# Weight slots as separate buffers at four different places within 512 bytes, in a hybrid mLSTM, retention and FFN layer on one core

## The reference, cut to what matters

```
h    = rmsnorm(x, g_mix_pre)
proj = h @ w_in                       # 2048 x 8208: q, k, v, gates of 8 mLSTM and 8 retention heads
mix  = concat(mlstm heads, retention heads) @ w_out            # 2048 x 2048
x    = x + rmsnorm(mix, g_mix_post)
h    = rmsnorm(x, g_ffn_pre)
ff   = (silu(h @ w_gate) * (h @ w_up)) @ w_down                # 2048 x 5632 twice, 5632 x 2048
x    = x + rmsnorm(ff, g_ffn_post)
```

## The kernel before, in words

| buffer | before | after |
|---|---|---|
| raw | 128 | 128 |
| w_hi, slots 0, 1, 2, 3 | 128, 128, 128, 128 | 128, 256, 384, 0 |
| w_lo, all slots | 128 | 0 |
| resid, columns, right, stat | 128 | 0 |
| hT, mixT, wg_both, qT, kT, gT | 0 | 384 |
| ffT, h2T, ff_g, ff_u, decay, v_sb, mixed | 384 | 256 |

## Time and profile before

### The profile page before, as it was taken

The page is one execution under the profiler, slowest core; times in us unless marked ns, Lnnn a source line. Parts: engine busy times, 40 slices in busy tenths (PEclk is TensorE's granted clock), DMA queues, the critical chain, the costliest instruction groups (busy, mean ns, idle before and its releaser), DMA issues.

```text
span 1277.3 us, 17523 instructions
## 1 busy us (share of the span) xinstructions
PE 1242.5 (97%) x6551; PEld 1060.9 (83%) x6551; DVE 761.2 (60%) x983; ACT 619.5 (48%) x817; POOL 13.8 (1%) x37
## 2 busy tenths in 40 slices
PE   4899999999999999999999999999999999999997
PEld 3688788888888888888888888888888888888886
DVE  2654667867777645666656666556656654444444
ACT  3553467565464744554444444444444443434432
POOL 2000010000000000000000000000000000000000
PEclk8999999999999999999999999999999999999999
DMA  8875778876878555365555555565565565555551
GB/s 113 226 218 121 169 167 184 187 155 157 198 161 194 197 186 181 127 198 188 177 194 186 176 196 182 179 197 177 185 197 174 187 230 193 189 193 185 197 197 66
DMA packets 183956, 229.42 MB, mean 180 GB/s; under 512 B 3888, under 2 KB 143408, under 8 KB 183408
## 3 DMA queue, kind: packets, MB, share of 16 engines
q1 hardware_dynamic: 183536, 226.70, 60.3%
q0 software_dynamic: 384, 2.23, 1.9%
HBM read 226.82 MB, written 2.10 MB: 179 GB/s over the span
## 4 chain that ended last, share of the span: by engine, by line
PE 90%; DMA 7%; DVE 2%; SPq 1%; ACT 0%; issue 0%; DVEq 0%; ACTq 0%
PE bank L1027 89%; DMA raw<-in_w_in 7%; DVE w_lo L642 1%; DVE h2T L649 0%; DVE resid L920 0%; ACT w_hi L396 0%; PE bank L1169 0%; SPq L302 0%; SPq L290 0%; ACT h2T L412 0%; SPq L297 0%; ACT bank L554 0%; PE bank L1032 0%; DVEq L118 0%; DVE ff_out L913 0%
## 5 line engine op out<-in xcount | busy, mean ns | idle before, releaser
L642 DVE TENSOR_TENSOR w_lo<-raw,w_hi 128x1024 fp32r<-128x1024 f32 x424 | 517.8, 1224 | 453.1 <-ACT w_hi L396 447.9
L396 ACT ACTIVATE w_hi<-raw 128x1024 fp32r<-128x1024 f32 x424 | 447.2, 1059 | 547.3 <-PE bank L1027 494.9
L1027 PE MATMUL bank<-h2T,w_hi 128*128 128x512 f32 x1408 | 497.9, 399 | 1.8 <-issue 1.6
L1027 PE MATMUL bank<-h2T,w_lo 128*128 128x256 f32 x1408 | 395.4, 281 | 0.0
L1027 PEld LDWEIGHTS bank<-h2T,w_hi 128*128 128x128 f32 x1408 | 264.5, 188 | 68.3 <-issue 1.8
L1027 PE MATMUL bank<-hT,w_hi 128*128 128x512 f32 x768 | 274.6, 398 | 0.5 <-DVE w_lo L642 0.5
L1027 PEld LDWEIGHTS bank<-h2T,w_lo 128*128 128x128 f32 x1408 | 266.0, 189 | 0.0
L1027 PE MATMUL bank<-hT,w_lo 128*128 128x256 f32 x768 | 217.7, 283 | 0.0
L1027 PE MATMUL bank<-w_hi,ffT 128*128 128x512 f32 x704 | 217.0, 389 | 0.0
L1027 PEld LDWEIGHTS bank<-hT,w_hi 128*128 128x128 f32 x768 | 145.0, 189 | 33.2 <-issue 0.7
L1027 PEld LDWEIGHTS bank<-w_hi,ffT 128*128 128x128 f32 x704 | 132.1, 188 | 27.7
(11 more groups left out here) (161 smaller groups left out, 586.3 us busy)
## 6 DMA issues: line engine op xcount, KB each, us to landing
raw<-in_w_in SPq DMA_DIRECT2D x64, 1024.0 KB, 14.9
raw<-in_w_gate SPq DMA_DIRECT2D x44, 1024.0 KB, 5.0
raw<-in_w_up SPq DMA_DIRECT2D x44, 1024.0 KB, 5.1
raw<-in_w_down SPq DMA_DIRECT2D x44, 1024.0 KB, 5.0
raw<-in_w_out SPq DMA_DIRECT2D x16, 1024.0 KB, 5.1
resid<-in_x SPq DMA_DIRECT2D x2, 1024.0 KB, 6.0
out<-resid SPq DMA_DIRECT2D x8, 256.0 KB, 2.5
g_post<-in_g_mix_post POOLq DMA_DIRECT2D x1, 1024.0 KB, 7.2
```

The source lines that it names most:

```text
L396: act.activation(w_hi[:, s % AHEAD, :], raw[:, s // 2, (s % 2) * SUB:(s % 2 + 1) * SUB], ACT.Copy).then_inc(hi_done, 1)
L642: dve.tensor_tensor(w_lo[:, s % AHEAD, :], raw[:, s // 2, (s % 2) * SUB:(s % 2 + 1) * SUB], w_hi[:, s % AHEAD, :].bitcast(F32), ALU.subtra ...
L1027: return pe.matmul(out_, lhsT, rhs, start=start, stop=stop, skip_group_check=True)
```

## The change

`w_hi` and `w_lo` were one buffer each with four slots of 4096 bytes. Now each slot is a buffer of its own, and the code that names a slot calls `w_hi(slot, c0, c1)` or `w_lo(slot, c0, c1)`. The small buffer `floor` (128 bytes), which stood near the end of the mixer's buffers, now stands between slots 0 and 1 of `w_hi`; slots 2 and 3 are each 128 bytes longer at their front, which nothing uses (`gap`, 32 numbers). So the slots of `w_hi` begin 128 bytes further within 512 from one to the next, and all that stands behind them moves by 384 bytes; the table above has the places. Every engine issues the same instructions in the same order with the same waits and shapes; only operand addresses differ.

```diff
--- before.py
+++ after.py
@@ -47,6 +47,8 @@
 RAW_CHUNKS = 4
 AHEAD = 4
 
+SHIFT = 128
+
 R_V = 0
 R_IN = R_V + 4
 R_OUT = R_IN + 12
@@ -124,8 +126,19 @@
 
 
         raw = sb("raw", [P, RAW_CHUNKS, 2 * SUB])
-        w_hi = sb("w_hi", [P, AHEAD, SUB], F32R)
-        w_lo = sb("w_lo", [P, AHEAD, SUB], F32R)
+        gap = SHIFT // 4
+        hi_slots = [sb("w_hi0", [P, SUB], F32R)]
+        floor = sb("floor", [P, TT, 2 * HEADS])
+        hi_slots += [sb(f"w_hi{n}", [P, SUB + (gap if n > 1 else 0)], F32R) for n in range(1, AHEAD)]
+        lo_slots = [sb(f"w_lo{n}", [P, SUB], F32R) for n in range(AHEAD)]
+
+        def w_hi(slot, c0=0, c1=SUB):
+            skip = gap if slot > 1 else 0
+            return hi_slots[slot][:, skip + c0:skip + c1]
+
+        def w_lo(slot, c0=0, c1=SUB):
+            return lo_slots[slot][:, c0:c1]
+
         resid = sb("resid", [P, TT, D])
         columns = sb("columns", [P, 2, P])
         ident, coef = columns[:, 0, :], columns[:, 1, :]
@@ -161,7 +174,6 @@
         cosT = sb("cosT", [P, SEQ], stack=mixer)
         sinT = sb("sinT", [P, SEQ], stack=mixer)
         a_col = sb("a_col", [P, TT, HEADS], stack=mixer)
-        floor = sb("floor", [P, TT, 2 * HEADS], stack=mixer)
         vec = sb("vec", [P, 4], stack=mixer)
         mixer.close()
         new = pre[:, :, CONV - 1:]
@@ -393,7 +405,7 @@
 
                 rnd, s = rnd + s // 8, s % 8
                 act.wait_ge(raw_full[s // 2], 16 * (rnd + 1))
-                act.activation(w_hi[:, s % AHEAD, :], raw[:, s // 2, (s % 2) * SUB:(s % 2 + 1) * SUB],
+                act.activation(w_hi(s % AHEAD), raw[:, s // 2, (s % 2) * SUB:(s % 2 + 1) * SUB],
                                ACT.Copy).then_inc(hi_done, 1)
 
             def ahead(rnd, s):
@@ -639,8 +651,8 @@
 
                 rnd, s = rnd + s // 8, s % 8
                 dve.wait_ge(hi_done, 8 * rnd + s + 1)
-                dve.tensor_tensor(w_lo[:, s % AHEAD, :], raw[:, s // 2, (s % 2) * SUB:(s % 2 + 1) * SUB],
-                                  w_hi[:, s % AHEAD, :].bitcast(F32), ALU.subtract).then_inc(lo_done, 1)
+                dve.tensor_tensor(w_lo(s % AHEAD), raw[:, s // 2, (s % 2) * SUB:(s % 2 + 1) * SUB],
+                                  w_hi(s % AHEAD).bitcast(F32), ALU.subtract).then_inc(lo_done, 1)
 
             def transposed_lo(dst, gain, tiles0, tiles=range(KT)):
 
@@ -1041,9 +1053,9 @@
                 for c in range(2):
                     for j in range(4):
                         k = 4 * quarter + j
-                        cols = slice(256 * j + P * c, 256 * j + P * (c + 1))
-                        mm(bank[:, 2 * pair + c, :], w_hi[:, slot, cols], act_T[:, k, :], k == 0, False)
-                        ins = mm(bank[:, 2 * pair + c, 0:SEQ], w_lo[:, slot, cols], act_T[:, k, 0:SEQ],
+                        cols = 256 * j + P * c, 256 * j + P * (c + 1)
+                        mm(bank[:, 2 * pair + c, :], w_hi(slot, *cols), act_T[:, k, :], k == 0, False)
+                        ins = mm(bank[:, 2 * pair + c, 0:SEQ], w_lo(slot, *cols), act_T[:, k, 0:SEQ],
                                  False, k == KT - 1)
                 ins.then_inc(sub_done, 1)
 
@@ -1062,13 +1074,13 @@
 
                 pe.wait_ge(lo_done, count)
                 for j in range(2):
-                    k, w = k0 + j, slice(512 * j, 512 * (j + 1))
+                    k, w = k0 + j, (512 * j, 512 * (j + 1))
                     for t in tiles:
                         hi_x = act_T[:, k, t * P:(t + 1) * P]
                         lo_x = act_T[:, k, SEQ + t * P:SEQ + (t + 1) * P]
-                        mm(bank[:, 2 * pair + t, :], hi_x, w_hi[:, slot, w], k == 0, False)
-                        mm(bank[:, 2 * pair + t, :], hi_x, w_lo[:, slot, w], False, False)
-                        ins = mm(bank[:, 2 * pair + t, :], lo_x, w_hi[:, slot, w], False, k == last)
+                        mm(bank[:, 2 * pair + t, :], hi_x, w_hi(slot, *w), k == 0, False)
+                        mm(bank[:, 2 * pair + t, :], hi_x, w_lo(slot, *w), False, False)
+                        ins = mm(bank[:, 2 * pair + t, :], lo_x, w_hi(slot, *w), False, k == last)
                 if TT - 1 in tiles:
                     ins.then_inc(sub_done, 1)
                 return ins
```

## The result

| | median us | range, runs |
|---|---|---|
| kernel before | 1270.38 | 1267.88 to 1275.75, 10 |
| changed kernel | 1276.91 | 1274.47 to 1281.98, 10 |

The changed kernel takes 1.0049 times as long, 95% interval 1.0026 to 1.0073: 6.2 us slower, between 3.3 and 9.3. The forecast was no change (1271 us); the time lies inside its range.

The account below looks back on a forecast made before the run. PE bounds the kernel by product count times spacing, except DMA in the v stage. Terms -1.5 + 0.6 + 1.7 - 0.8 sum to 0.0 us, put on the runs' median: 1271 us, range 1262 to 1280.

Parts of the forecast that it names:

- term 1: FFN, 1408 pairs at 353.4 ns: three quarters go to 352 ns, -1.5 us, bounds -18 to +10.
- Term 3: w_down, 1056 products at 226.7 ns: 528 with moved w_hi go to 230 ns, +1.7 us.
- the reading by distance: All product stages: spacing is set by the stationary tile's place less the moving operand's, modulo 512 bytes.
- The 230 ns for an unknown distance: Token order: 230 ns a product assumed at unseen distances, from the gates' sweep over 16 places.
- Term 2: q and k, 768 pairs at 351.0 ns: three quarters go to 352 ns, +0.6 us, bounds -8 to +7.
- Term 4: w_out, 384 products at 232.8 ns: moved w_hi products go to 226.7 or 230 ns, -0.8 us.
- A: All stages, mixture: distance matters by a few ns, gains and losses cancel; 1269 to 1274 us, chance 0.33.
- Term 5: v stage: DMA ends it, so 0; another -0.8 us if that cover were gone.
- Terms 6 and 7: ACT and DVE durations unaffected by places, 0; calls, floor's new place and gap issue nothing, 0.
- B: FFN, q and k: spread breaks a locked stall pattern, 348 ns or less a pair; 1265 us, chance 0.28.
- D: All stages: places have no effect, all spacings stay, FFN pair 353.4 ns; 1271 us, chance 0.13.
- C: Good locks lost: w_down +4.8 us, q and k +1.4, FFN gains nothing; 1277 us, chance 0.26.

Follow-up runs that it names:

- experiment 7: Kernel before unchanged, 1267.48 us; and the kernel before with hT, mixT and h2T moved to classes 224, 0 and 32, 1268.46 us, ratio 1.0001.
- experiments 3 to 5: Against the kernel before: activations moved or w_hi slots spread separately, then spread by 256 bytes or mixer buffers moved 128, then activations at finer distances; ratios 0.9985 to 1.0088.
- experiments 3 and 4: Against the kernel before: activations moved 384 bytes (1.0067), w_hi slots spread alone (1.0057), slots spread by 256-byte steps (0.9999), mixer activations moved 128 bytes (0.9985).
- e_act: Kernel before with only the activations and all else behind the weights moved by 384 bytes; 1277.57 us, ratio 1.0067.
- before_third: Kernel before, unchanged, one more look for another draw of the FFN's pattern; 1267.48 us.
- experiment 2: The changed kernel, unchanged, measured and traced a second time; 1281.72 us, ratio 1.0096 to the kernel before.
- experiment 3: Parts of the change on the kernel before: activations alone moved 384 bytes, 1277.57 us (1.0067); w_hi slots alone spread, 1275.56 us (1.0057).
- e_spread: Kernel before with only the slots of w_hi spread (128, 256, 384, 0), w_lo and activations at their old places; 1275.56 us, ratio 1.0057.
- experiment 8: Kernel before with hT at class 224 and mixT at 0, ffT and h2T as before; 1263.60 us beside 1267.34, ratio 0.9972.
- e_combo: Kernel before with hT moved 160 bytes (class 224) and mixT 384 (class 0), ffT and h2T as before; 1263.60 us, ratio 0.9972.
- e_d64: Kernel before, weights unmoved, activations moved to distances modulo 256 of 64 (q and k, w_out) and 192 (FFN, v, w_down); 1282.19 us, ratio 1.0088.
- e_d32: Kernel before, weights unmoved, activations moved to distances modulo 256 of 224 (q and k), 32 (FFN, v, w_down), 96 (w_out); 1281.08 us, ratio 1.0088.
- e_mixer128: Kernel before with hT, mixT and all behind them in the mixer moved by 128 bytes, to distance 0; 1267.67 us, ratio 0.9985.
- before_again: Kernel before, unchanged, for a second trace and the spread of its runs; 1271.77 us, ratio 1.0012.
- e_hi128: Kernel before with all w_hi slots moved by the same 128 bytes against w_lo and the activations, modulo 256; 1274.83 us, ratio 1.0042.

## Why the prediction was wrong, step by step

I forecast no change, from four terms that cancel; the kernel became 6.2 us slower.

**The point that failed first: term 1, the base of the FFN.** It took the kernel's pair as 353.4 ns from one trace and got -1.5 us. That is the rarer of two patterns: both other traces of the kernel before have 346.9 ns, and 4 of 23 runs in experiment 7 lie in the upper group. The changed kernel has 350.8 in the mean of its slots, so the term is 1408 x 3.9 = +5.5 us against an ordinary execution. The sign is wrong because of the base: the 350.8 itself lies close to the 352 for moved and 353.4 for unmoved pairs.

**The step that hid it.** I wrote that the runs without the profiler end some 6 us below the span, and put the sum on the median. So a sum worked out from an execution with the 353.3 ns went onto the time of ordinary ones. The result lists time and span of one run together: 1274.82 and 1272.8, so a run is some 2 us *longer* than its span. The profiled execution of before had then taken about 1279 us (an estimate), 8 above the median of the runs shown, near the 9 us between the two patterns. The three runs lay within 2.4 us of each other, and the span stood 6 above their median in the first table; I gave no reason for it.

**Term 3, `w_down`.** +1.7 us was forecast; +2.9 came (242.5 against 239.6). Right in sign: this stage has the one good class, and `w_hi` leaves it. The size was off in two ways. Modulo 256 only slots 0 and 2 leave the class, not three quarters; and I left slot 3 and all products with `w_lo` at 226.7, while the pattern runs on across sub-tiles, so every slot pays: 229.0, 229.9, 229.0, 229.9. By my own sign the reading by distance was wrong if slot 3 changed, and it did: distance gives the steady spacing (experiments 3 to 5), but a slot's own distances don't fix its spacing when its neighbours differ.

**The 230 ns for an unknown distance.** The sweep over the gates' 16 places was read as the token order, but there `hT` moves and the weights are stationary. In the token order the two unknown distances are 0 with 226.7 and 128 with 232.4 (experiments 3 and 4). Their mean is near 230, which is luck: no distance measured has 230.

**Term 2, q and k.** +0.6 us was forecast. Slots 0 and 2, whose `w_hi` goes to class 0, fell to some 347 to 349 ns, and slots 1 and 3 stay at some 351. The heads' products interrupt this stage, and by how the interrupted sub-tiles are counted the mean is 348.6 to 349.7 against 351: -1.1 to -1.9 us. The sum below takes -1.1. **Term 4, `w_out`:** -0.8 forecast; 231.9 against 232.4, -0.2 us, and 90.1 us for the stage against 90.3 to 90.5. Slots 0 and 2, whose `w_hi` is at the good class, have 233.0 and slots 1 and 3 have 231.5, the opposite of what I gave as A's sign.

**Term 5, v.** It was 0 since a transfer ended the stage. That was again the one trace: after 58.7 us no transfer stands in the chain of the v stage in after, nor in the second and third trace of before, and e_act's v stage did get shorter with its spacing. The term came out near 0 (92.9 us against 92.6 and 93.1) because v's own mean hardly moved, 232.2 against 232.4. **Terms 6 and 7** held: ACT and DVE have the same durations, and the order of instructions is the same.

**The sum.** 5.5 + 2.9 - 1.1 - 0.2 = 7.1 us against an execution with the fast FFN. before_third (span 1265.5) and the first trace of after (1272.8) differ by 7.3. That the two agree so well is partly luck: with -1.9 for q and k the sum is 6.3, and in time q and k took the same in these two traces (296.6 and 296.5 us), while from trace to trace they vary with their transfers by 8 us (up to 304.4). If one run in six of before loses 9 us (4 of 23 in experiment 7), the means differ by 1.5 less, 5.6; both lie within the measured 3.3 to 9.3. The 12 us of experiment 2 don't follow from this sum.

**The rivals.** None gave the FFN's 350.7: A wanted 352 to 353, B 348 or less, D 353.4, C more. A (the stages cancel) fell. B counted on three quarters of the pairs gaining from a pattern that the switches break; the switches do break it, but the pattern they break is mostly the good one. C named one of the right stages and its loss, the good lock of `w_down`, and the time it gives (1277) is the measured one, but that is luck: its +4.8 for `w_down` was +2.9, its +1.4 for q and k was a gain, and the FFN, which it left as it was, brought most of the loss. What it lacked is that the FFN has a good lock to lose too. D is shown wrong by experiment 3: 384 bytes of shift alone move `w_out` from 232.4 to 227.0 and `w_down` from 226.7 to 232.4. So the Trainium skill's rule ("TensorE: Matmul & The Clock Gate", Part 2: loading the next tile doesn't steal bandwidth from the running matmul) does not describe this kernel, if it is read to say that addresses are free: the spacing moves by up to 7.6 ns in 227 with the class alone. What I took for distance modulo 512 is modulo 256, which also spoils my counts of "unknown" distances: class 0 and 128 were both in the rows.

**What stays open.** Which part of the chip makes two reads of one engine meet like this wasn't tried; that it is the two reads is my reading, and what the runs show is that the spacing follows the distance. Nor was a shift of weights and activations together by the same odd amount, so that only the distance counts rests on `w_down`'s slots in after and in e_spread, which have the same classes at other places and the same spacings. Why a slot of class 0 pays behind one of a mixed class isn't explained either. Why the FFN goes one way or the other after its last foreign products, and the share of each, is open too: the kernel before had 4 runs of 23 in the upper group beside experiment 7 and none in 15 beside experiment 8.

## What to carry to other kernels

Before you sum terms on a trace, check that it is of an ordinary execution: put its span beside the timed runs, and take an unexplained gap of half a per cent as a finding, not as overhead. In a kernel that TensorE bounds, read the start-to-start spacing of products; where the same shape has two values in two stages, compare the byte places of its two operands modulo 256, and give every pair the class that measures best instead of spreading the slots (here 0 in the token order; in the column order 224 for q and k and 0 for the FFN, as in e_combo, since 0 and 32 can also fall into 353.3 ns a pair). A steady rhythm can have more than one form for one layout, so a few runs say little about differences below 1%.

## What the runs showed of the hardware that was not expected

- The spacing of back-to-back float32r products of 512 columns is 226.7 to 234.3 ns at the full clock, by the distance of stationary and moving operand modulo 256 bytes. From the best to the worst class that is 3.4% in the token order; `w_down` takes 239.6 us at class 0 and 246.6 at 32. And e_d64 and e_d32, which changed nothing but places, lost 0.9% of the whole, the FFN's slow value included.
- One and the same instruction stream runs in one of two exact rhythms, 346.9 or 353.3 ns a pair, for 490 us on end; it changes where short foreign products stand between (the heads' work in q and k of e_act and e_mixer128, the first rounds of the FFN).
- ACT's writes to `w_hi` and DVE's reads of it don't show in PE's spacing. In the FFN of the first trace of before, pairs wholly beside an ACT copy have 353.35 ns in the mean and those wholly clear of one 353.34; for DVE's subtraction 353.32 and 353.35. In before_again, e_d64 and e_hi128 the two means differ by 0.4 ns at most.
